# A second, unread 512-column product behind each product for the first head's maxima

## The reference, cut to what matters

```python
hl = mod_norm(xl, norm_g[i], sh_l, sc_l)
s = (jnp.einsum('bqhd,bkhd->bhqk', qn, k_nope) + jnp.einsum('bqhr,bkr->bhqk', qr, k_rope)) * scale
p = jax.nn.softmax(s, axis=-1)                   # MLA; GQA and SWA have one einsum, SWA a band and a sink
o = jnp.einsum('bhqk,bkhd->bqhd', p, v)
xl = xl + gt_l * (o * jax.nn.silu(gate)) @ w_out[i]
```

## Time and profile before

| | us |
|---|---|
| median of 3 runs | 4576.33 |
| lowest and highest | 4575.15, 4577.26 |
| the profiled execution | 4586.22 |
| its span, first to last instruction | 4584.4 |
| PE busy in the span | 4033.1 (88%) |
| DVE busy | 2720.6 (59%) |
| ACT busy | 2383.3 (52%) |
| mean granted clock of PE, as a share of full speed | 0.945 |

### The profile page before, as it was taken

The page is one execution under the profiler, slowest core; times in us unless marked ns, Lnnn a source line. Parts: engine busy times, 40 slices in busy tenths (PEclk is TensorE's granted clock), DMA queues, the critical chain, the costliest instruction groups (busy, mean ns, idle before and its releaser), DMA issues. The chain is left out here.

```text
span 4584.4 us, 62659 instructions
## 1 busy us (share of the span) xinstructions
PE 4033.1 (88%) x21052; PEld 1968.6 (43%) x21052; DVE 2720.6 (59%) x3726; ACT 2383.3 (52%) x3194; POOL 1236.1 (27%) x875
## 2 busy tenths in 40 slices
PE   5996799999988979999988978888889778999998
PEld 1453244444444443444444544444444333444444
DVE  4324577777446447777745427777543336777754
ACT  2324367777433237777722216766423345777761
POOL 1000144343222114444412102322210102444442
PEclk8998799999999989999999979999999888999999
DMA  4125432223111332222111332333111353122211
GB/s 194 44 71 146 126 73 63 69 61 72 53 33 52 99 91 73 72 72 72 48 58 53 108 108 73 87 92 86 54 32 64 91 153 74 42 51 51 51 40 56
DMA packets 375200, 345.00 MB, mean 75 GB/s; under 512 B 252576, under 2 KB 290016, under 8 KB 373392
## 3 DMA queue, kind: packets, MB, share of 16 engines
q1 hardware_dynamic: 375056, 343.12, 27.2%
HBM read 251.82 MB, written 91.23 MB: 75 GB/s over the span
## 5 line engine op out<-in xcount | busy, mean ns | idle before, releaser
L696 PE MATMUL bank<-H_hilo,w_hilo 128*128 128x512 f16 (+1 forms) x6336 | 1158.8, 346 | 28.2 <-DVE w_hilo L910 25.9
L1431 DVE TENSOR_REDUCE max_parts<-bank 128x1 f32<-128x512 f32 (+2 forms) x1536 | 955.2, 652 | 276.6 <-PE bank L1376 235.2
L1618 ACT ACTIVATE p_f<-bank 128x1024 f32<-128x1024 f32 (+2 forms) x768 | 742.2, 966 | 577.5 <-PE bank L1572 550.6
L1572 PE MATMUL bank<-q_slots,k_slots 96*128 96x512 f16 (+7 forms) x3968 | 944.5, 368 | 1.0 <-ACT p_hi L1622 0.8
L1690 DVE TENSOR_TENSOR p_lo<-p_f,p_hi 128x1024 f16<-128x1024 f32 (+2 forms) x624 | 742.5, 1193 | 278.5 <-ACT p_hi L1622 274.4
L696 PEld LDWEIGHTS bank<-H_hilo,w_hilo 128*128 128x128 f16 x6336 | 622.7, 98 | 566.5 <-DVE w_hilo L910 27.5
L1622 ACT ACTIVATE p_hi<-bank 128x1024 f16<-128x1024 f32 (+2 forms) x768 | 738.0, 961 | 0.0
L1376 PE MATMUL bank<-k_slots,q_slots 96*128 96x512 f16 (+4 forms) x1536 | 527.9, 382 | 137.6 <-DVE max_parts L1431 77.7
L1544 PE MATMUL bank<-p_hi,v_hi_ones 128*128 128x512 f16 (+2 forms) x1568 | 567.9, 363 | 6.2 <-DVE o_f L1670 2.6
L1546 PE MATMUL bank<-p_hi,v_lo_zeros 128*128 128x512 f16 (+2 forms) x1568 | 567.7, 362 | 0.0
L1548 PE MATMUL bank<-p_lo,v_hi_ones 128*128 128x512 f16 (+2 forms) x1568 | 567.0, 363 | 0.0
(11 more groups left out here) (164 smaller groups left out, 3472.2 us busy)
## 6 DMA issues: line engine op xcount, KB each, us to landing
ada_w<-in_w_ada SPq DMA_DIRECT2D x48, 768.0 KB, 5.6
k_slots<-k_gqa SPq DMA_DIRECT2D x96, 224.0 KB, 4.5
gate<-z_ring SPq DMA_DIRECT2D x32, 640.0 KB, 2.9
gate_rows<-gate SPq DMA_DIRECT2D x64, 320.0 KB, 4.0
q_slots<-q_mla SPq DMA_DIRECT2D x64, 240.0 KB, 3.3
k_mla<-hilo_out SPq DMA_DIRECT2D x64, 224.0 KB
k_slots<-k_mla SPq DMA_DIRECT2D x64, 224.0 KB, 4.4
v_hi_ones<-v_scratch SPq DMA_DIRECT2D x64, 224.0 KB, 2.9
```

What stands on the lines that cost most here:

```text
L696: ins = pe.matmul(dst, lhs(a, k), rhs(b, k), start=(k == 0 and n == 0), stop=(k == nk - 1 and n == 2))
L1431: dve.tensor_reduce(mx[:, par, t, c:c + 1], MB[(b * NE + k) % 2][:, 0:n], AX.X, ALU.max).then_inc(s_red.h, 1)
L1572: ins = pe.matmul(dst, lhs, rhs, start=(m == 0), stop=(m == len(ops) - 1), skip_group_check=swa)
L1618: act.activation(p32[:, p % 2, 0:cols], src, ACT.Exp, scale=scale).then_inc(s_p32.h, 1)
```

## The change

Behind each product of a max entry in the lead-in stands a second product of 512 columns. It takes the first 128 queries and the first 512 keys of the first head, with 96 rows in MLA and 64 in GQA and SWA, and writes a whole output bank, `OB[0]` and `OB[1]` in turn. It waits for nothing, signals nothing, and nothing reads what it writes. The entries in the loop are as before. That makes 26 + 26 + 18 + 26 = 96 more products, each with its weight load.

```diff
                 pe.wait_ge(s_ld[0].h, s_ld[0].base + 16 * n_loads)
                 for k in range(NE):
                     emit_entry(pe, 0, 0, k)
+                    if entries[k][0] == "max":
+                        pe.matmul(OB[k % 2], Q[0:mrow, 0, 0, 0:P], K[0:mrow, 0, 0, 0:BANK], start=True, stop=True)
```

## The result

| | us, median (lowest to highest) | runs |
|---|---|---|
| before, timed beside it | 4578.36 (4571.52 to 4586.79) | 20 |
| changed | 4591.77 (4575.43 to 4600.54) | 20 |
| ratio changed / before | 1.0027, 95% interval 1.0018 to 1.0035 | |
| profiled execution, before / changed | 4586.22 / 4594.48 | |

The forecast was 4568.6, the range 4562 to 4579. The changed kernel is about 12 us slower by the ratio (0.27% of 4578) and 13.4 by the medians, and its median lies outside the range.

A forecast was written before the change was run, and what follows sets the result against it. PE was taken as slow at each attention's start, its low clock paid four times, with slow-product latency in the lead-in's ring; lead-ins and loops summed to -7.7 us, 4576.33 to 4568.6 us, range 4562 to 4579.

The forecast's parts named there:

- The step that failed: Lead-ins at the low clock: an entry with its addition takes PE 0.86 us, without pause, costing 0.16 us an entry.
- The second rival: Lead-ins: the clock doesn't rise at all and the additions are plain load, +14.0 us, 4590.3; chance 0.08.
- The lead-ins of layers 0 and 1: Additions cost 0.9 us until the clock rises, then entries go at DVE's pace: together -0.9 us in each layer.
- DVE's stall: Lead-ins of layers 0 and 1, after the first products: DVE's small operation on the negated maxima takes 2.22 us.
- Layer 3: Lead-in of layer 3: a DVE operation slips into POOL's second fill, the clock rises later: together -1.0 us.
- Layer 2: Lead-in of layer 2, with more small waits: clock rises for a while, low again at the loop; 0, ends -1 and +2.6.
- The loops: Loop starts to the first value product at the high clock: -2.2 us in layer 0, -0.8 in layer 1, -1.9 in layer 3.
- the first rival: Clock falls again in the last wait before the loop in layers 0, 1 and 3: -2.2 us, 4574.1; chance 0.17.
- The sum: Whole kernel: lead-ins -0.9 - 0.9 - 1.0 + 0 and loops -2.2 - 0.8 - 1.9 make -7.7 us.
- A quarter of 0.53: The share of the main forecast's 0.53 chance lying beyond the 9.2 us a measurement can tell, counted as faster.
- the third rival: Layer 2 gains as well, or the clock rises within 3 us everywhere: -10 to -11 us, 4566; chance 0.17.
- The pace at the high clock: Lead-ins after the clock's rise: entries go at DVE's pace, 0.61 us apart instead of 0.70.

The follow-up runs named there:

- the second profile: The changed kernel timed and profiled once more with no further edit: 4589.99 us, ratio 1.0023 to before.

## Why the prediction was wrong, point by point

- **The step that failed:** "An entry with its addition takes PE 0.86 us at the low clock", with "With the additions at the low clock PE has no pause". In layers 1 and 2 the entry takes 1.08, and the 0.11 us ahead of each product is the pause that had been ruled out. I took 0.43 from loops whose score products have 128 and 65 rows, and named the 64 rows in a rival only as work. The row that would have priced a change to 64 rows didn't exist in the trace, and I gave it no bound.
- The second rival had the sign, and nearly the size: it said +14.0 for no rise anywhere. That the size fits is luck: it priced layer 1's lead-in at +3.5 and layers 0 and 3 at +3.5 and +4.4, and they measured +7.4, +0.8 and +0.8. The rise failed in two layers of four, for a reason which it had only in part.
- The Trainium skill, TensorEngine Tiling (Array Packing), section "Key Properties", says that a change of the tiling mode drains TensorE; its section "Available Configurations" lists arrays of 64 and of 32 rows as modes beside the one of 128. The prediction left this rule out. The runs agree where they reach: +0.11 us at each change (at the low clock), none from 64 to 64. That this time is such a drain no run shows.
- **"The lead-ins of layers 0 and 1"**: -0.9 each. Layer 0 measured +0.8 and, in the second profile, -1.1; the mechanism is there. The forecast counted the time to the rise from the end of DVE's stall, 5.0 us (the mean of three loops; with layer 2's 8.0 it would be 5.7). Measured from there it is 12.5 us in the first profile and 4.0 in the second. Layer 1 measured +7.4; with 128 rows it is -2.2.
- **Layer 3**: -1.0 forecast, +0.8 measured: the rise came 11.2 us into the lead-in (12.8 in the second profile), not 5.0. The third 512-column entry came where it was forecast, 3.2 us in. The held DVE operation came as predicted. DVE, then POOL, at the start of layer 3's lead-in, changed kernel:

```profile
3801.44 1.41 DVE L1442 TENSOR_SCALAR neg_max<-max_rows 128x2 f16<-128x2 f32 x1
```
```profile
3801.23 1.58 POOL L1715 MEMSET v_lo_zeros<- 128x1792 f16 x1
```

  It takes 1.41 us instead of the 0.19 of the earlier trace rows, and ends with POOL's fill.
- **Layer 2**: 0 forecast, with +2.6 as the end; +4.1 measured, the same cause; with 128 rows it is -0.9.
- **The loops**: layer 3 -1.9 forecast and measured. Layer 0 -2.2 forecast, -0.9 measured in the first profile, because the clock fell in the last wait of 1.08 us (the first rival; the stretch 544.30 to 547.80 above is at 0.51); where it didn't, in the run with MLA alone, the loop's start took 4.9, as worked out. Layer 1 -0.8 forecast; +0.6 with the change, -0.8 with 128 rows.
- **The sum** was nearly right for another kernel, the one with 128 rows: -7.3 by its account (lead-ins -3.3, loop starts -4.0) against -7.7. In part this is luck, since layers 1 and 2 gain more there than forecast and layers 0 and 3 less.
- A quarter of 0.53 and the third rival's 0.17 make 0.30, not 0.31; nothing hangs on it.
- **The pace at the high clock** was right: with 128 rows layer 1's products stand 0.60 us apart (1678.52, 1679.12, 1679.72), DVE's own pace.

What stays open: with 65 rows the account of the profile gives 4 us (110.1 against 114.1), the medians 12.0. The profiled execution was the slowest of its eight (4581.33, of 4560.69 to 4581.33), 4.9 below before's profile. How often the clock rises early in the other seven wasn't seen. Among the kernels with 65 rows or more in every layer, none is told from another by its total: the steps behind the 128 rows are seen in the profiles alone.

## What to carry to other kernels

- An unread product that is meant to keep TensorE's clock up should take more than half of the array's rows where its neighbours do: with 64 or 32 rows it cost over 7 us in a lead-in of 22, with 65 or 128 the kernel as a whole became 0.2 to 0.3% faster. Look at the distance of the starts, not at the busy share, which showed 97% for the stream with gaps.
- Look for the waits behind which the clock falls (the end of the phase ahead, a wait on another engine, the last wait before the dense part), and not only for places where products already stand. Filling them kept the clock up in the profiles; that it shortens the whole launch further, the totals don't show.
- Where a forecast rests on a stride, take it from rows with the same row counts in turn; a count that no row has is an unknown with two bounds.

## What the runs showed of the hardware that was not expected

- A weight load lies beside the running product for 96 behind 96, 128 behind 128, 65 and 128 in turn, and 64 behind 64 (starts 0.40 to 0.43 us apart at 1.2 GHz). Between 128 and 64, 96 and 64, or 128 and 32 rows it is not, and the next start is 0.11 us later at each change.
- A lead-in at 0.43 us a product, broken only by waits for DVE, needed 4 to 16 us to the rise, 7.7 and 16.2 in the same layer of the same kernel; with 0.54 us it didn't rise in 27 to 30 us, nor in 40 with twice the products.
- At 1.00 a PE wait of 1.08 us ahead of four transposes ended with the clock at 0.50 in layer 0 and at 1.00 in layer 3 of one and the same execution. Behind an idle of 2.03 or 2.06 us it fell 1.0 us into the next stream, though products were running again.
